# Residual affine work between the late blocks, an earlier load of its vectors, a later transpose in one tail, and waits for one block

## The reference

```
# first network: post-norm, twice
x = layer_norm(ALPHA * x + mixer(x),    ln_mix_g[i], ln_mix_b[i])   # mixer 0: short conv + SSD, mixer 1: forgetting attention
x = layer_norm(ALPHA * x + conv_ffn(x), ln_ffn_g[i], ln_ffn_b[i])
def layer_norm(x, g, b): return (x - mean) * rsqrt(var + eps) * g + b
def conv_ffn(x): h = causal_conv3(x @ w_up) + conv_b; u, g = split(h); return (u * silu(g)) @ w_down
# second network: pre-norm, twice
mod = silu(c) @ ada_w[i] + ada_b[i]            # 6 vectors of 1024: shifts, scales, gates
h = rmsnorm(x, norm1_g[i]) * (1 + sc1) + sh1
x = x + g1 * mixer2(h)                         # mixer2 0: grouped attention, mixer2 1: chunked gMLP
h = rmsnorm(x, norm2_g[i]) * (1 + sc2) + sh2
x = x + g2 * (relu(h @ w_in) ** 2) @ w_out
```

## Time and profile before

| what | value |
|---|---|
| median of three runs | 2961.83 us |
| the profiled execution's own time | 2962.14 us |
| its span in the trace | 2960.1 us |
| TensorE (PE) busy | 2827.4 us, 96% |
| GpSimd (POOL) busy | 1157.5 us, 39% |
| VectorE (DVE) busy | 1376.3 us, 46% |
| ScalarE (ACT) busy | 1077.9 us, 36% |
| mean granted TensorE clock | 0.976 |

### The profile page before, as it was taken

One profiled execution on the slowest core, in us unless ns is written; L12 is line 12 of the kernel. 1 busy time (PEld: TensorE's weight loads), 2 busy tenths in 40 slices (PEclk: granted clock), 3 DMA queues, 4 the chain that ended last, 5 costly groups with the idle time before them and its releaser, 6 DMA issues.

```text
span 2960.1 us, 37222 instructions
## 1 busy us (share of the span) xinstructions
PE 2827.4 (96%) x13518; PEld 2303.0 (78%) x13518; DVE 1376.3 (46%) x1548; ACT 1077.9 (36%) x1520; POOL 1157.5 (39%) x472
## 2 busy tenths in 40 slices
PE   7998798999999988999979999999999999999999
PEld 6787587888878767888857677888878888878887
DVE  4432837885255446886346654122242633331232
ACT  4322243333344343434343544233442223432332
POOL 3442043444434203544424213435434434434443
PEclk9999799999999999999989999999999999999999
DMA  5332024763233103873313002323233222223222
GB/s 145 92 93 71 1 92 151 247 220 99 86 93 93 43 15 106 263 238 110 100 57 98 1 29 84 94 92 100 95 116 109 79 81 90 93 85 99 93 93 78
DMA packets 314367, 297.76 MB, mean 101 GB/s; under 512 B 11980, under 2 KB 246680, under 8 KB 314136
## 3 DMA queue, kind: packets, MB, share of 16 engines
q1 hardware_dynamic: 299832, 235.64, 26.4%
q10 hardware_dynamic: 14432, 60.70, 6.0%
HBM read 294.21 MB, written 2.10 MB: 100 GB/s over the span
## 4 chain that ended last, share of the span: by engine, by line
PE 42%; issue 38%; POOL 15%; DVE 2%; ACT 1%; POOLq 0%; ACTq 0%; DVEq 0%
POOL wlo L526 15%; PE ps L1927 7%; PE ps L1928 7%; PE ps L1929 7%; PE ps L1817 6%; PE ps L1818 5%; PE ps L1819 5%; PE ps L2238 1%; PE ps L2125 1%; PE ps L2098 1%; DVE rowst L1532 1%; ACT pbuf L848 1%; DVE alo L1337 1%; PE ps L1951 0%; PE ps L1953 0%
## 5 line engine op out<-in xcount | busy, mean ns | idle before, releaser
L526 POOL TENSOR_TENSOR wlo<-raw,whi 128x1024 fp32r<-128x1024 f32 x444 | 1132.2, 2554 | 1762.1 <-ACT whi L584 1761.7
L1817 PE MATMUL ps<-xhi,whi 128*128 128x512 f32 x1824 | 722.2, 396 | 25.8 <-DVE gt L1456 10.2
L1818 PE MATMUL ps<-xlo,whi 128*128 128x512 f32 x1824 | 715.9, 392 | 0.0
L1819 PE MATMUL ps<-xhi,wlo 128*128 128x512 f32 x1824 | 715.3, 392 | 0.0
L584 ACT ACTIVATE whi<-raw 128x1024 fp32r<-128x1024 f32 x444 | 466.1, 1051 | 344.1 <-PE ps L1929 172.0
L1927 PE MATMUL ps<-whi,ahi 128*128 128x512 f32 x1184 | 464.9, 393 | 10.2 <-issue 7.8
L1928 PE MATMUL ps<-wlo,ahi 128*128 128x512 f32 x1184 | 463.1, 391 | 0.0
L1929 PE MATMUL ps<-whi,alo 128*128 128x512 f32 x1184 | 463.0, 391 | 0.0
L1817 PEld LDWEIGHTS ps<-xhi,whi 128*128 128x128 f32 x1824 | 346.0, 190 | 100.6 <-issue 21.8
L1819 PEld LDWEIGHTS ps<-xhi,wlo 128*128 128x128 f32 x1824 | 345.9, 190 | 72.9
L1818 PEld LDWEIGHTS ps<-xlo,whi 128*128 128x128 f32 x1824 | 346.3, 190 | 70.2
(11 more groups left out here) (280 smaller groups left out, 2938.4 us busy)
## 6 DMA issues: line engine op xcount, KB each, us to landing
adaraw<-in_ada_w ACTq DMA_DIRECT2D x64, 768.0 KB, 6.0
raw<-in_ffn_w_up SPq DMA_DIRECT2D x88, 512.0 KB, 3.9
raw<-in_mlp_w_in SPq DMA_DIRECT2D x64, 512.0 KB, 4.0
raw<-in_mlp_w_out SPq DMA_DIRECT2D x64, 512.0 KB, 3.5
raw<-in_gmlp_w_in SPq DMA_DIRECT2D x48, 512.0 KB, 3.8
raw<-in_sc_ssm_w_in SPq DMA_DIRECT2D x44, 512.0 KB, 3.8
raw<-in_ffn_w_down SPq DMA_DIRECT2D x44, 512.0 KB, 3.6
raw<-in_fox_w_in SPq DMA_DIRECT2D x24, 512.0 KB, 3.8
```

What stands on the lines that cost most here:

```text
L526: pool.tensor_tensor(wlo[:, j], raw[:, j], whi[:, j].bitcast(F32), ALU.subtract).then_inc(w_lo, 1)
L1817: pe.matmul(out, lh, rh, start=start, stop=False)
L1818: pe.matmul(out, lh, rl, start=False, stop=False)
L1819: return pe.matmul(out, ll, rh, start=False, stop=stop)
```

## The change

Four edits, all of order and waits; the same arithmetic is done.

1. `dve_resid` is cut up and called from inside `dve_xt`, after each of the blocks 3 to 7: two multiplications after block 3, one instruction after each of blocks 4, 5 and 6, three after block 7.
2. `load_gb` moves from behind `act_xt` to the end of `act_ln_tail`, behind the last standard deviation.
3. In `pe_t_tail`, for q = 4, tile 0 of the normed rows is transposed behind tile 3's matmuls, no longer ahead of them.
4. `pe_t_unit` gets a wait for one block in front of each of its two halves; `pe_qkv` and `pe_gm` use it in place of the wait for two blocks.

```
-    def act_ln_tail(act, r, name):
+    def act_ln_tail(act, r, name, g_ap, b_ap):
...
             if t == 1:
                 act_next_whi(act, name, 2)
+        load_gb(act, gb, g_ap, b_ap)
...
-        act_ln_tail(act, 0, "out0")
+        act_ln_tail(act, 0, "out0", a["ln_mix_g"][0:1], a["ln_mix_b"][0:1])
         act_xt(act, 1, lambda k: col("lnm0g", k), lambda k: col("lnm0b", k))
-        load_gb(act, gb, a["ln_mix_g"][0:1], a["ln_mix_b"][0:1])
...
-    def dve_xt(dve, q):
+    def dve_xt(dve, q, resid=None):
...
             dve.tensor_tensor(xlo[:, k], xf[:, k % 2], xhi[:, k].bitcast(F32), ALU.subtract).then_inc(xt_lo, 1)
+            if resid is not None:
+                dve_resid(dve, resid, k)
...
+    def dve_resid(dve, r, k):
+
+        def scale(t):
+            dve.tensor_tensor(xres[:, t], nrm[:, t], gb[:, 0], ALU.mult).then_inc(res_mul, 1)
+
+        def shift(t):
+            dve.wait_ge(res_mul, 4 * r + t + 1)
+            dve.tensor_tensor(xres[:, t], xres[:, t], gb[:, 1], ALU.add).then_inc(res_done, 1)
+
+        if k == 3:
+            dve.wait_ge(gb_in, 32 * (r + 1))
+            dve.wait_ge(nrm_done, 8 * r + 8)
+            scale(0)
+            scale(1)
+        if k == 4:
+            shift(0)
+        if k == 5:
+            scale(2)
+        if k == 6:
+            shift(1)
+        if k == KD - 1:
+            scale(3)
+            shift(2)
+            shift(3)
...
-        dve_xt(dve, 1)
-        dve_resid(dve, 0)
+        dve_xt(dve, 1, resid=0)
...
-    def pe_t_unit(pe, start, e, j, bank0, lh, ll, first):
+    def pe_t_unit(pe, start, e, j, bank0, lh, ll, first, blocks=None):
...
         for k in range(2):
+            if blocks is not None:
+                pe.wait_ge(xt_lo, blocks + k + 1)
...
-            if q and t == 2 and i:
+            if q and q != 4 and t == 2 and i:
                 pe_xt_tile(pe, q, 0)
         if q:
-            for t in range(1, NT):
+            for t in range(0 if q == 4 else 1, NT):
                 pe_xt_tile(pe, q, t)
...
         for j in range(4):
-            pe.wait_ge(xt_lo, 48 + 2 * j + 2)
-            unit(0, j, 1)
+            unit(0, j, 1, blocks=48 + 2 * j)
```

More of the change, by code:

```diff
@@ L1079, in _ @@
         act_jit(act, "out0", ya_yb, head=act_out0_head)
-        act_ln_tail(act, 0, "out0")
+        act_ln_tail(act, 0, "out0", a["ln_mix_g"][0:1], a["ln_mix_b"][0:1])
         act_xt(act, 1, lambda k: col("lnm0g", k), lambda k: col("lnm0b", k))
-        load_gb(act, gb, a["ln_mix_g"][0:1], a["ln_mix_b"][0:1])
         act_ffn(act, 0)
         act_jit(act, "dn0", hid_ff, head=ffn_head(0))
-        act_ln_tail(act, 1, "dn0")
+        act_ln_tail(act, 1, "dn0", a["ln_ffn_g"][0:1], a["ln_ffn_b"][0:1])
         act.dma_start(wf_raw[:], w_fox[:, :, 3 * D:3 * D + 16]).then_inc(small_in, 16)
         act_xt(act, 2, lambda k: col("lnf0g", k), lambda k: col("lnf0b", k))
-        load_gb(act, gb, a["ln_ffn_g"][0:1], a["ln_ffn_b"][0:1])
         act.wait_ge(small_in, 16 * 6)
@@ L1098, in _ @@
         act_jit(act, "fo", oT1)
-        act_ln_tail(act, 2, "fo")
+        act_ln_tail(act, 2, "fo", a["ln_mix_g"][1:2], a["ln_mix_b"][1:2])
         act_xt(act, 3, lambda k: col("lnm1g", k), lambda k: col("lnm1b", k))
-        load_gb(act, gb, a["ln_mix_g"][1:2], a["ln_mix_b"][1:2])
         act_ffn(act, 1)
@@ L1764, in _ @@
         dve_ln_tail(dve, 1, "dn0")
-        dve_xt(dve, 2)
+        dve_xt(dve, 2, resid=1)
         dve.wait_ge(wf_hi, 2)
         dve.tensor_tensor(wf_lo_t[:], wf_raw[:], wf_hi_t[:].bitcast(F32), ALU.subtract).then_inc(wf_lo, 1)
-        dve_resid(dve, 1)
         assert dve_soft(dve, fl_dve, fl_act, 2, small[:, 3], False, sm[:, 9]) == 12
@@ L1774, in _ @@
         dve_ln_tail(dve, 2, "fo")
-        dve_xt(dve, 3)
-        dve_resid(dve, 2)
+        dve_xt(dve, 3, resid=2)
         dve_ffn(dve, 1)
@@ L2165, in units @@
             for j in js:
-                pe_t_unit(pe, S + 4 * h, j, j, 4 * ((h + 1) % 2), xhi[:, 2 * j:2 * j + 2], xlo[:, 2 * j:2 * j + 2], j == 0)
+                pe_t_unit(pe, S + 4 * h, j, j, 4 * ((h + 1) % 2), xhi[:, 2 * j:2 * j + 2], xlo[:, 2 * j:2 * j + 2], j == 0,
+                          blocks=None if h else 32 + 2 * j)
         pe.wait_ge(res_add, 32)
         for j in range(4):
-            pe.wait_ge(xt_lo, 32 + 2 * j + 2)
             units(0, [j])
@@ L2226, in pe_gm, with unit @@
         S, SU = U0["gv"], U0["gu"]
-        def unit(e0, j, b):
-            pe_t_unit(pe, S, e0 + j, j, 4 * b, xhi[:, 2 * j:2 * j + 2], xlo[:, 2 * j:2 * j + 2], j == 0)
+        def unit(e0, j, b, blocks=None):
+            pe_t_unit(pe, S, e0 + j, j, 4 * b, xhi[:, 2 * j:2 * j + 2], xlo[:, 2 * j:2 * j + 2], j == 0, blocks=blocks)
         def spatial(cc):
```

## The result

The changed kernel took 2938.0 us in the median of four runs (2936.66 to 2939.23), beside 2962.64 us (2960.99 to 2963.56) for the kernel before, measured in turns on the same chip: a ratio of 0.9917, with a 95% interval from 0.99 to 0.9935. The profiled execution took 2937.71 us with a span of 2935.8 us, where before it was 2962.14 and 2960.1. The forecast was 2938.5, in a range of 2933.5 to 2947. Lines have moved: 1822 is 1833, 1817 is 1828, 1927 is 1940, 1456 is 1470, 1435 is 1432, 1150 is 1148.

The account below looks back on a forecast made before the run. TensorE, busy 96% of the span, was taken to bound the kernel. Gains of 7.0 + 6.9 + 7.3 + 2.1 = 23.3 us off the median of 2961.83 gave 2938.5 us, range 2933.5 to 2947.

Parts of the forecast that it names:

- Edits 1 and 2 in the up projections: TensorE's stall for `gt` before unit 4 goes, with the slow stretch behind it: 7.0 and 6.9 us.
- the clock part: Behind the unit 4 stall, the first nine matmuls take 3.75 us where nine at full clock take 2.04.
- The meeting with GpSimd: VectorE's last residual instructions meet GpSimd's low part of unit 3; cost 0 to 0.3 us, twice, taken as 0.
- My two cases: At unit 3's low part: VectorE loses up to 2.2 us, margin 4; or GpSimd loses, ending at 484.4, cover used up.
- Unit 6: Up projections: high and low parts, behind two modulation loads, ready at 497 to 499.5; TensorE asks at 500.7, margin 1 to 4.
- first rival: Up projections stall again at unit 6, behind the modulation loads: 2952.4 us, or 2945.5 for half; chance 0.12.
- r = 1: Stretch between the up projections: residual work off the path, three loads before the first block; 0, at worst 0.3 us.
- Edit 3: Double norm's tail: VectorE's 7.29 us wait for tile 3 goes and everything after shifts; gain 7.3, bounds 6.5 and 7.3.
- the lower bound: Double norm's tail: gain of 6.5 us instead of 7.3 if ScalarE's last standard deviation, behind a norm, costs its 0.7.
- Edit 4: Products behind the double norm and norm 6: TensorE starts on block 0, 1.1 us earlier each; 2.1 taken, bounds 0 and 2.3.
- my lower bound of the edit: Products behind the double norm and norm 6: gain 0 if the slow stretch merely ends by the same moment.
- some 2 us of shifts in the stages behind: Allowance in the edges of the forecast's 2934.5 to 2942 us, for stages behind the changes.

Follow-up runs that it names:

- fill_wait: Kernel before, with 21 matmuls nobody reads put into TensorE's wait ahead of unit 4 of both up projections; 2956.72 us, 0.9981.
- load_only: Kernel before, with `gb` loaded at the tail's end and the residual step left in one piece behind block 7; 2958.83 us, 0.9987.
- blocks_only: Kernel before, with only the wait for two blocks replaced by one wait for each block inside the unit; 2958.48 us, 0.9988.
- gb_after_3: Changed kernel, with `gb`'s two loads issued later, behind ScalarE's block 3; 2939.4 us, 0.9923 of the kernel before.
- gb_after_4: Changed kernel, with `gb`'s two loads issued later, behind ScalarE's block 4; 2949.33 us, 0.9958 of the kernel before.
- resid_only: Changed kernel with the double norm's transpose order and the one-block waits undone; 2948.41 us, 0.9952 of the kernel before.
- tail_only: Kernel before, with only tile 0 of the double norm transposed behind tile 3's matmuls; 2954.55 us, 0.9973.
- warm_tail: Changed kernel with matmuls nobody reads in TensorE's waits of the seven norm tails; 2923.47 us, 0.987 of the kernel before.

## Why the prediction was right

**Bound and method.** TensorE bounds both kernels, and each wait that was removed from it came back in the time. The trace gave 24.3 us against 23.3.

**Edits 1 and 2 in the up projections (7.0 and 6.9).** Measured 7.0 and 7.1, and 14.1 with these edits alone. The two parts of the term were tested apart: the clock part, 1.7 to 1.9 each, is what fill_wait gives (1.6 and 1.8). The steps held as counted. Block 4's low part ends at 470.5, TensorE asks at 475.7, a margin of 5.2 (forecast 5.0). `gb` is there at 460.23 + 5.7 = 465.9, which is 466.3 in the time of the kernel before, as forecast. The second `gb` load took 5.3 to 5.7 us to land where it took 4.9 to 5.4; at the first place it took 0.3 us more, with a load of the weight ring now beside it, and no instruction waits for that. The ring load felt it more: the 512 KB unit issued there landed after 6.9 us, where it had taken 3.9 alone; no instruction waited for that either. The Trainium skill, page DMA: Bandwidth & Descriptors, section "Issuing engines are not separate DMA queues", has the loads interleave, and these landings agree in kind.

**The meeting with GpSimd (0, at worst 0.3).** It came. GpSimd's low part took 3.26 us instead of 2.40, VectorE's last pair 4.55 instead of 2.4. Unit 3's low part stood at 482.48 and TensorE asked at 484.00, so 1.5 us of cover were left and nothing was paid. My two cases had the one engine or the other lose. The rows show both losing, one turn each: VectorE 2.2 us, its worst case, and GpSimd 0.9, as it did not stand behind all three instructions. GpSimd starts at 479.22 beside an addition that began at 479.01, ends at 482.48, and VectorE's next addition ends 1.1 us later, at 483.56.

The Trainium skill, page SBUF — State Buffer, section "Who interferes with whom", says that whoever issues first holds the shared ports for its whole instruction while the other stands still. It fits these rows: by the rule and the rows' durations GpSimd would end at about 479.01 + 1.2 + 2.4 = 482.6, an estimate, and 482.48 was measured.

**Unit 6 (margin 1 to 4, first rival).** VectorE did wait for the modulation loads, 1.3 and 1.2 us, as the rival said, but unit 6's high and low parts stood by about 497 and TensorE asked at 500.3: a margin of 3. The landing was 5.1 to 7.7 us here, not 8.4.

**r = 1 (0, at worst 0.3).** -0.2 us over 411 us of stages. The traces show where: the last eight transposes of that norm take 1.97 us, where the kernel before has 1.31. The three loads ahead of the first block, which I had as the risk, are not the cause, for load_only issues the same three and has 1.31 there.

**Edit 3 (7.3).** Measured 7.4 in the whole change and alone. ScalarE's 0.7 us, the lower bound, were not paid.

**Edit 4 (2.1).** Measured 1.1 and 0.9, alone 1.1 and 1.1. The half unit on block 0 hid block 1's arrival, as counted, and TensorE's first matmul came 1.0 us earlier behind block 0 at both places. Behind norm 6 that gain stayed. Behind norm 4 one step of mine did not hold, "the late transposes, the blocks and the weights behind them follow from that start". The slow stretch behind the start grew from nine matmuls to thirteen, and the late transposes stand 9.1 us behind the start of block 0's low part where they stood 9.2. Unit 0 in windows, before and after:

```profile
1549.40:1556.80 7.40, 7.40 (x25) 5.93 (x26) 1.96 (x4) 0.77 (x1) 0.00 (x0) 0.74 0.00 0
...
1526.70:1534.90 8.20, 8.20 (x24) 6.48 (x25) 2.94 (x6) 1.50 (x2) 0.00 (x0) 0.65 0.00 0
```

So at that point my lower bound of the edit, 0, had nearly come true. The time came back later, in the attention between 1628 and 1640. There all four kernels with edit 4 (the changed one, blocks_only, gb_after_3, gb_after_4) reach 1.1 us for this edit, after 0.2 to 0.6 ahead of it; the four that lack it (resid_only, tail_only, load_only and fill_wait) reach 0.1 or less either way. The size is therefore the edit's, but at norm 4 not by the route I gave, and why the attention returns it was not found.

**What the sum did not have.** 0.4 at the start, 0.6 between 1785 and 1980, and -0.2 in r = 1, all within what kernels do in stages where they don't differ. My "some 2 us of shifts in the stages behind" was of that size. That it came out small is chance, and of the 0.5 us between forecast and median I make nothing.

**Where I was wrong**, beside the step of edit 4, was in an expectation: load_only. I carried the removed wait through as if VectorE's work behind it kept its length, though the prediction had priced such a meeting at 2.2 us. And I took the clock to fall, or not, alike at both places.

## What to carry to other kernels

Price a stall of the bounding engine as its idle time plus the slow stretch behind it, and look for the work that stands ahead of the release: here spreading it over gaps that its engine already had gave 7.0 us a place together with the early input, and the early input alone 3.3 and 0.8. When an instruction starts earlier, ask which instruction of the other engine it now meets; here a VectorE and a GpSimd operation that both read SBUF took 2.2 of the 3.8 us that an earlier start had won. Where a wait can't be removed, unread matmuls inside it gave back the clock's share of it (1.6 and 1.8 us in fill_wait).

## What the runs showed that I had not expected

- Two stalls of 3.45 us in one execution, with the same units on both sides, were followed by a granted clock of 1.00 in one place and 0.50 in the other. The stall of 5.1 us had 0.56 behind it. What decides in between was not settled.
- A short instruction paid nearly as much as a long one when GpSimd was ahead of it: block 7's 0.69 us low part took 2.77 and 2.73 us, 2.1 and 2.0 more, and a 1.2 us multiplication 2.2 more.
- Filling TensorE's waits in seven tails (warm_tail) gave 14.5 us, 0.5% of the time, for 128 matmuls that nobody reads.
- Kernels that are the same up to the first norm reach it up to 2.3 us apart (the first mean and variance step of that norm starts 0.6 us before to 1.7 us behind that of the kernel before, over nine traces), and between 1785 and 1980 they differ by up to 1.3 us. It is most of why three parts measured by themselves sum to 26.1 us and the whole to 24.6. For the stage at 1800 the traces show what differs: how many matmuls behind the norm run 0.43 us apart before the distance falls to 0.23. The kernel before has such distances for 5.7 us, the changed one for 4.0. The first 6 us of that product, before and after:

```profile
1800.10:1806.10 6.00, 5.95 (x17) 4.78 (x17) 3.10 (x7) 2.33 (x3) 0.00 (x0) 0.52 0.01 3
...
1777.40:1783.40 6.00, 5.92 (x20) 4.75 (x21) 3.49 (x7) 2.33 (x3) 0.00 (x0) 0.65 0.01 3
```

So the shift is a clock that rises at another moment. What sets the moment was not found.
